# A decoder layer in fp32r halves: another order of work at the ends of parts, at the entry and in the tail

## The reference, cut to what matters

```python
x = x + 0.5 * swiglu(rmsnorm(x, ffn1_norm), ffn1_gate, ffn1_up, ffn1_down)   # 2048 -> 5632 -> 2048
u = rmsnorm(x, mix_norm) @ w_in                       # 8 projections: 4 differential heads, 8 stick-breaking heads
x = x + concat(diff_attention(u), stick_breaking(u)) @ w_out
x = x + 0.5 * swiglu(rmsnorm(x, ffn2_norm), ffn2_gate, ffn2_up, ffn2_down)
x = rmsnorm(x, final_norm)
```

## Time and profile before

| | us |
|---|---|
| median of 3 runs (lowest, highest) | 1858.45 (1858.03, 1859.05) |
| the profiled execution, its own time | 1858.01 |
| span of its trace, first to last instruction | 1856.2 |
| TensorE busy (share) | 1840.0 (99%) |
| VectorE busy | 1029.1 (55%) |
| ScalarE busy | 834.2 (45%) |
| GpSimd busy | 16.1 (1%) |
| mean granted TensorE clock | 0.998 |
| share of time of the 16 transfer engines | 58% |

### The profile page before, as it was taken

How to read it: one execution, slowest core, us unless ns; L and a number is a source line. 1 busy time by engine, 2 the same in 40 slices (tenths; PEclk the granted TensorE clock), 3 DMA queues, 4 the chain that set the end, 5 groups by cost and what they waited for, 6 DMA issues and landing times.

```text
span 1856.2 us, 21845 instructions
## 1 busy us (share of the span) xinstructions
PE 1840.0 (99%) x8490; PEld 1532.9 (83%) x8490; DVE 1029.1 (55%) x1135; ACT 834.2 (45%) x1059; POOL 16.1 (1%) x18
## 2 busy tenths in 40 slices
PE   9999999999999999999999999999999999999998
PEld 7888788888888887888888888888888888888887
DVE  6555545455545457655665576555544555554565
ACT  6434333444334445554656445434333434343444
POOL 0000000000000000101000000000000000000000
PEclk9999999999999999999999999999999999999999
DMA  8656555555656646654445466656565556566653
GB/s 315 208 197 213 193 192 198 196 195 196 224 187 210 206 155 217 216 177 163 159 162 179 147 217 216 213 197 212 193 202 189 195 196 208 198 236 221 201 169 115
DMA packets 230445, 365.78 MB, mean 197 GB/s; under 512 B 13920, under 2 KB 91488, under 8 KB 230368
## 3 DMA queue, kind: packets, MB, share of 16 engines
q1 hardware_dynamic: 229792, 363.78, 58.2%
q10 hardware_dynamic: 576, 0.96, 0.1%
HBM read 346.85 MB, written 2.10 MB: 188 GB/s over the span
## 4 chain that ended last, share of the span: by engine, by line
PE 56%; issue 38%; SPq 2%; DVE 2%; DMA 1%; POOL 0%; ACT 0%; POOLq 0%; DVEq 0%
PE psum L1549 46%; PE psum L1451 5%; PE psum L1456 2%; SPq L414 2%; DMA w_raw<-in_ffn_up 1%; DVE w_split L892 0%; DMA lo_sum<-head_out 0%; DVE x_res L1402 0%; POOL head_rstd L496 0%; DVE x_res L1091 0%; DVE head_out L1127 0%; PE psum L1679 0%; SPq L462 0%; PE psum L1725 0%; PE psum L1694 0%
## 5 line engine op out<-in xcount | busy, mean ns | idle before, releaser
L892 DVE TENSOR_TENSOR w_split<-w_raw,w_split 128x1024 fp32r<-128x1024 f32 (+1 forms) x656 | 764.8, 1207 | 614.3 <-ACT w_split L531 612.8
L1549 PE MATMUL psum<-w_split,x_split 128*128 128x512 f32 x4752 | 1083.7, 390 | 1.8 <-DVE w_split L973 1.8
L531 ACT ACTIVATE w_split<-w_raw 128x1024 fp32r<-128x1024 f32 (+1 forms) x660 | 656.2, 1042 | 920.3 <-PE psum L1549 875.6
L1549 PEld LDWEIGHTS psum<-w_split,x_split 128*128 128x128 f32 x4752 | 891.0, 188 | 187.2 <-DVE w_split L973 2.6
L1549 PE MATMUL psum<-w_split,h_split 128*128 128x512 f32 x2208 | 503.5, 389 | 2.5 <-DVE h_split L1018 2.2
L1549 PEld LDWEIGHTS psum<-w_split,h_split 128*128 128x128 f32 x2208 | 413.9, 188 | 90.1 <-issue 3.7
L1451 PE MATMUL psum<-x_split,w_split 128*128 128x512 f32 x256 | 80.0, 396 | 0.0
L1044 DVE SCALAR_TENSOR_TENSOR strip_sum<-psum,rstd_tok,normed 128x512 f32<-128x512 f32 x44 | 31.0, 747 | 45.5 <-PE psum L1549 45.5
L1456 PEld LDWEIGHTS psum<-x_split,w_split 128*128 128x128 f32 x256 | 46.9, 188 | 10.6
L1451 PE MATMUL psum<-h_split,w_split 128*128 128x512 f32 x168 | 51.8, 395 | 0.0
L1456 PE MATMUL psum<-x_split,w_split 128*128 128x256 f32 x256 | 49.1, 278 | 0.0
(11 more groups left out here) (180 smaller groups left out, 553.8 us busy)
## 6 DMA issues: line engine op xcount, KB each, us to landing
w_raw<-in_ffn_gate SPq DMA_DIRECT2D x87, 1024.0 KB, 5.1
w_raw<-in_ffn_up SPq DMA_DIRECT2D x87, 1024.0 KB, 5.2
w_raw<-in_ffn_down SPq DMA_DIRECT2D x76, 1024.0 KB, 5.1
w_raw<-in_w_in SPq DMA_DIRECT2D x48, 512.0 KB, 4.7
w_raw<-in_w_in SPq DMA_DIRECT2D x24, 1024.0 KB, 5.1
w_raw<-in_w_out SPq DMA_DIRECT2D x16, 1024.0 KB, 5.1
lo_sum<-head_out SPq DMA_DIRECT2D x480, 32.0 KB, 1.9
w_raw<-in_ffn_down SPq DMA_DIRECT2D x16, 768.0 KB, 4.7
```

Of the source, the lines that this page charges most:

```text
L531: nc.scalar.activation(w_split[:, slot % 2, 0, h * half:(h + 1) * half], w_raw[:, slot, h * half:(h + 1) * half], ACT.Copy).then_inc(hi_ma ...
L892: nc.vector.tensor_tensor(w_split[:, slot % 2, 1, part], w_raw[:, slot, part], w_split[:, slot % 2, 0, part].bitcast(F32), ALU.subtract).t ...
L1549: ins = mm(psum[:, bank + t, :], x[:, a, t * P:(t + 1) * P], w[:, b, k, :], start=kk == 0 and (a, b) == (0, 0), stop=kk == count - 1 and a ...
```

## The change

It does the following.

- **Entry.** Two dummy products in place of three. `first_pair` takes high x high, low x high, high x low (x's half is named first), and waits for x's low half and the weights' low half only where they are used. Chunk 2 comes in two halves with a semaphore each; ScalarE and VectorE split chunk 2, then chunk 3.
- **Moves.** At the end of an all-moved part SP issues 12 of the 16 small transfers and ScalarE the other 4 (`move_last_quarter`), ahead of its next conversion.
- **Parts of three chunks.** In VectorE's list `x_from_moved` of the group before now stands after the new delta and the chunk's low half at `q == 2`; `group_norm` on ScalarE and `group_x_lo`, `group_sums` on VectorE stand later by a group, and in the mixer's first chunk groups 2 and 3 are done one by one (`group_high`, `group_squares`).
- **Norm.** VectorE adds the two rows of `square_sum` (`fold_sum`), and TensorE takes two products in place of four, in all norms but the last.
- **Tail.** VectorE scales blocks 3 to 15 in six parts. TensorE spreads the factor into a second bank as well, ScalarE copies it to SBUF, and GpSimd scales blocks 0 to 2 with it (`POOL_PART`). ScalarE issues their output before its last part's.

The diff without its unchanged lines and the two semaphore declarations, indented less:

```diff
@@ -230,7 +230,8 @@
-OUT_PARTS = ((0, 1), (1, 3), (3, 6), (6, 9), (9, 12), (12, 14), (14, 16))
+OUT_PARTS = ((3, 4), (4, 6), (6, 9), (9, 12), (12, 14), (14, 16))
+POOL_PART = (0, 3)
@@ -406,10 +409,10 @@
-        def move_turned(count):
+        def move_turned(count, quarters=4):
...
-            for q in range(4):
+            for q in range(quarters):
@@ -431,7 +434,7 @@
-                    move_turned(count)
+                    move_turned(count, 3 if ph["g0"] is not None and ph["all_moved"] and count == ph["last_moved"] else 4)
@@ -464,8 +467,13 @@
-                for w in range(2):
-                    group_chunk(0, j + w)
+                if j == 2:
+                    dst = w_raw[:, 2, :].rearrange("p (k n) -> p k n", n=2 * STRIP)
+                    for h, done in enumerate((half_landed, landed[2])):
+                        sp.dma_start(dst[:, 2 * h:2 * h + 2, :], source(0, 1)[:, 2 * h:2 * h + 2, :]).then_inc(done, 16)
+                else:
+                    group_chunk(0, j)
+                group_chunk(0, j + 1)
@@ -484,7 +492,7 @@
-    sp.wait_ge(out_written, 16 * len(OUT_PARTS))
+    sp.wait_ge(out_written, 16 * (len(OUT_PARTS) + 1))
@@ -518,6 +526,11 @@
+    pool.wait_ge(x_hi_made, 8 * NORM_FINAL + NS)
+    pool.wait_ge(norm_ready, 2)
+    lo, hi = POOL_PART
+    nc.gpsimd.tensor_tensor(x_blocks[:, lo:hi, :], x_blocks[:, lo:hi, :],
+                            rstd[:, :].unsqueeze(1).broadcast_to([P, hi - lo, T]), ALU.mult).then_inc(pool_scaled, 1)
@@ -561,7 +574,7 @@
-            act.wait_ge(squares_added, q + n)
+            act.wait_ge(squares_added, q + 2 * n)
@@ -595,13 +608,16 @@
-    for c in (2, 3):
-        act.wait_ge(landed[c], 16)
-        act.wait_ge(entry_used, c - 1)
-        hi_part(c, c, HALF_K, 0)
-    for c in (2, 3):
-        act.wait_ge(chunk_used, c + 1)
-        hi_part(c, c, HALF_K, 1)
+    act.wait_ge(half_landed, 16)
+    act.wait_ge(entry_used, 1)
+    hi_part(2, 2, HALF_K, 0)
+    act.wait_ge(landed[2], 16)
+    act.wait_ge(chunk_used, 3)
+    hi_part(2, 2, HALF_K, 1)
+    act.wait_ge(landed[3], 16)
+    act.wait_ge(chunk_used, 4)
+    for h in range(2):
+        hi_part(3, 3, HALF_K, h)
@@ -652,6 +668,25 @@
+    def group_high(ph, i):
+        act.wait_ge(res_done, ph["r0"] + i + 1)
+        for j in range(2):
+            x_hi_parts(2 * i + j, ph["norm"])
+    def group_squares(ph, i):
+        n = ph["norm"]
+        for j in range(2):
+            if i < 3:
+                act.wait_ge(squares_added, 8 * n + 2 * i + j + 2 * n)
+            nc.scalar.activation((normed if i == 3 else squares)[:, j, :, :], x_res[:, 2 * i + j, :, :],
+                                 ACT.Square).then_inc(squared, 1)
+    def move_last_quarter(count):
+        act.wait_ge(hidden_32, count)
+        for a in range(4):
+            act.dma_start(hidden_moved[96:128, a, :, :, :], turned_32[32 * a:32 * a + 32, 3, :, :, :]).then_inc(hidden_landed, 16)
@@ -660,18 +695,22 @@
+                elif i + q == 0:
+                    move_last_quarter(ph["last_moved"])
...
-                if q == 2 and i and ph["norm"] is not None:
+                if ph["norm"] is not None and ph["chunks"] == 4 and q == 2 and i:
...
+                if ph["norm"] is not None and ph["chunks"] == 3 and q == 0 and i > 1:
+                    group_norm(ph, i - 2)
...
-            act.wait_ge(squares_added, 8 * n + NS - 1 + n)
+            act.wait_ge(squares_added, 8 * n + NS - 1 + 2 * n)
@@ -860,9 +899,13 @@
+                if cc == 0:
+                    group_high(ph["after"], 2)
...
-                    group_norm(ph["after"], 3)
+                    group_high(ph["after"], 3)
+                    group_squares(ph["after"], 2)
+                    group_squares(ph["after"], 3)
@@ -872,6 +915,12 @@
+        if n == 0:
+            act.wait_ge(norm_spread_done, 3)
+            nc.scalar.activation(rstd[:, :], psum[:, 7, 0:T], ACT.Copy).then_inc(norm_ready, 1)
+        if n == 5:
+            act.wait_ge(pool_scaled, 1)
+            act.dma_start(out_t[:, slice(*POOL_PART), :], x_blocks[:, slice(*POOL_PART), :]).then_inc(out_written, 16)
@@ -910,13 +959,17 @@
-        dve.wait_ge(squares_added, q + n + 1)
+        dve.wait_ge(squares_added, q + 2 * n + 1)
...
+    def fold_sum(n):
+        dve.wait_ge(squares_added, 10 * n + 9)
+        nc.vector.tensor_tensor(square_sum[:, 0, :], square_sum[:, 0, :], square_sum[:, 1, :], ALU.add).then_inc(squares_added, 1)
@@ -966,12 +1019,8 @@
-    for h in range(2):
-        for c in (2, 3):
-            dve.wait_ge(hi_made, 4 + 2 * h + c - 1)
-            part = slice(h * 4 * STRIP, (h + 1) * 4 * STRIP)
-            nc.vector.tensor_tensor(w_split[:, c % 2, 1, part], w_raw[:, c, part], w_split[:, c % 2, 0, part].bitcast(F32),
-                                    ALU.subtract).then_inc(lo_made, 1)
+    for c in (2, 3):
+        lo_parts(c, c, HALF_K)
@@ -1069,6 +1118,7 @@
+                    fold_sum(0)
@@ -1078,6 +1128,8 @@
+        if i == 3:
+            fold_sum(ph["norm"])
@@ -1117,7 +1169,7 @@
-                if q == 1 and i and ph["turns"]:
+                if i and ph["turns"] and q == (ph["chunks"] - 1 if ph["chunks"] == 3 else 1):
@@ -1134,7 +1186,7 @@
-                if q == 0 and i > 1 and ph["norm"] is not None:
+                if q == (1 if ph["chunks"] == 3 else 0) and i > 1 and ph["norm"] is not None:
@@ -1375,9 +1427,9 @@
+                    group_x_lo(ph["after"], 2)
...
-                    group_x_lo(ph["after"], 2)
@@ -1408,7 +1460,7 @@
-    for _ in range(3):
+    for _ in range(2):
@@ -1477,14 +1529,15 @@
-        pe.wait_ge(squares_added, 9 * n + (8 if n == NORM_FINAL else 9))
+        pe.wait_ge(squares_added, 10 * n + (8 if n == NORM_FINAL else 10))
...
+        parts = 2 if n == NORM_FINAL else 1
...
-            for b in range(2):
-                ins = add(square_sum[:, b, :], t, b == 0, n != NORM_FINAL and b == 1)
+            for b in range(parts):
+                ins = add(square_sum[:, b, :], t, b == 0, n != NORM_FINAL)
@@ -1532,13 +1585,13 @@
-    def wide_chunk(c, slot, bank, quarter, left=None, count=KB, waits=None, during=None, second_lo=1):
+    def wide_chunk(c, slot, bank, quarter, left=None, count=KB, waits=None, during=None):
...
-                pe.wait_ge(lo_made, lo_value(c) - 1 + k // 2 * second_lo)
+                pe.wait_ge(lo_made, lo_value(c) - 1 + k // 2)
@@ -1556,12 +1609,15 @@
-            pe.wait_ge(x_ready if k % 2 else entry_x_ready, k // 2 + 1)
...
-                pe.wait_ge(*((lo_made, LO_CREDIT + 4) if k == 3 and w else (entry_lo, 2 * k + w + 1)))
+                pe.wait_ge(*((hi_made, 4) if k == 3 and w else (entry_hi, 2 * k + w + 1)))
...
-                for a, b in ((0, 0), (0, 1), (1, 0)):
+                for a, b in ((0, 0), (1, 0), (0, 1)):
+                    if a and w == 0:
+                        pe.wait_ge(x_ready if k % 2 else entry_x_ready, k // 2 + 1)
+                    if b:
+                        pe.wait_ge(*((lo_made, LO_CREDIT + 4) if k == 3 and w else (entry_lo, 2 * k + w + 1)))
@@ -1571,7 +1627,7 @@
-            wide_chunk(j, j, 2 * (j % 2), j // 2, waits=x_waits(0) if j % 2 == 0 else None, second_lo=2 if j == 2 else 1)
+            wide_chunk(j, j, 2 * (j % 2), j // 2, waits=x_waits(0) if j % 2 == 0 else None)
@@ -1785,10 +1841,11 @@
-    for b in range(2):
-        ins = mm(psum[:, 6, b * P:(b + 1) * P], rstd_tok[:, b:b + 1].broadcast_to([P, P]), const("ident"),
-                 start=True, stop=True)
-    ins.then_inc(norm_spread_done, 1)
+    for bank in (6, 7):
+        for b in range(2):
+            ins = mm(psum[:, bank, b * P:(b + 1) * P], rstd_tok[:, b:b + 1].broadcast_to([P, P]), const("ident"),
+                     start=True, stop=True)
+        ins.then_inc(norm_spread_done, 1)
```

More of the change, by code:

```diff
@@ L243, in hybrid_layer @@
         piece_landed = [sem(f"piece_landed{n}") for n in range(6)]
+        half_landed = sem("half_landed")
         x_block_landed = [sem(f"x_block_landed{n}") for n in range(2)]
@@ L282, in hybrid_layer @@
         out_ready = sem("out_ready")
+        pool_scaled = sem("pool_scaled")
         lam_ones = sem("lam_ones")
```

## The result

| | before | changed |
|---|---|---|
| median, us | 1858.33 | 1849.06 |
| lowest to highest (5 runs each) | 1858.03 to 1859.05 | 1848.72 to 1849.40 |
| ratio, 95% interval | | 0.995 (0.9939 to 0.9962) |
| profiled execution: its time, span | 1858.01, 1856.2 | 1849.11, 1847.3 |
| TensorE busy | 1840.0 | 1837.7 |

It is faster by 9.3 us, 0.50%. The forecast was 1850.8 with 1849.3 as its low end: the direction was right and the forecast mechanisms show in the rows, but more was won than the range allowed.

What follows compares the result with a forecast made beforehand. TensorE was busy 1840.0 of 1856.2 us, so only its idle or needless time could be won. Gains 2.4 + 1.2 + 2.2 + 1.9 + 0 = 7.7 off 1858.01, plus 0.44 for the median: 1850.8 us, range 1849.3 to 1854.5.

Steps and rivals of the forecast that it cites:

- The stock of stalls: TensorE's four listed waits in places the change touches: 5.9 us, nearly all stalls ahead of the tail.
- the moves: Ends of all-moved parts: with 12 issues SP is through 2.5 us earlier, removing three waits; gain 2.2 us, bounds 0 and 2.2.
- the seam: Third part into mixer: delta ahead of the moved addition, ready 2 us before the turn; gain 1.9 us, bounds 1.2 and 1.95.
- Median: 0.44 us added at the end: the profiled execution was 1858.01, the median of the runs shown 1858.45.
- Norm sums: Four records in place of eight at three norms, 0.4 us each; gain 1.2 us, bounds -0.3 and 1.2.
- Tail: Output scaling: counted at zero because the output's transfers set the end; bounds -0.3 and +0.87 us.
- Entry: Kernel start: first product 0.80 us earlier, chunk 4 at 27.3 instead of 29.7; gain 2.4 us, bounds 1.2 and 3.0.
- ScalarE's share of the issues: End of an all-moved part: its four issues, 2.5 us, fall in 3.49 us of idle time; it resumes about 188.6.
- Rival A: Small transfers: both queues together take no less than one did, the moves gain nothing: 1853.0 us; chance 0.12.
- C: Tail: GpSimd's multiplication is slow, each us beyond 3.6 delays the end; at 6 us 1853.2; chance 0.04.
- D: Entry: chunk 2's first half lands no earlier, chunk 4 at 28.5, entry gain 1.2: 1852.0 us; chance 0.10.
- B: Entry: TensorE's clock rise slips, products cost 0.43 instead of 0.23 us; eight such give 1851.8, all 96 1869; chance 0.10.

Runs made afterwards that it cites:

- u_moves: The changed kernel with SP issuing all 16 small transfers again and ScalarE none: 1852.33 us, 3.3 slower than the changed kernel.
- u_fold: The changed kernel without the fold, TensorE's norm sums taking eight records again at three norms: 1850.44 us, 1.4 slower.
- u_tail: The changed kernel with the tail put back (VectorE scales all 16 blocks, no GpSimd, no copy, one spread): 1849.11 us, the same.
- u_entry: The changed kernel with the whole entry put back (three dummies, old product order, chunk 2 whole, halves by turns): 1851.21 us, 2.15 slower.
- u_half: The changed kernel with chunk 2 in one transfer again, all else kept: 1850.47 us, 1.4 slower.

## Why the prediction was wrong, point by point

- **The stock of stalls** was the mis-sized term, and the step that failed. The forecast took the lines of the earlier trace rows as the cost of the stalls: 2.2 for the moves and 1.9 for the seam. In the profiled executions they cost 3.20 and 2.44, by the starts of products. Each listed stall was undercounted by about 0.25 us, and small losses (0.18 at one place of before, 0.36 ahead of the mixer with the seam back) were not listed at all. That is 1.54 us. u_moves shows it at four places. That records overlap was known ahead of the forecast, and was not applied to the waits.
- **Range.** For the moves I took 2.2 as the upper bound, the sum of the list, and for the seam 1.95. A bound read from a list that undercounts is no bound, and so the low end stood 0.24 us too high. So small a distance is within the tenths by which sets differ; the 1.7 us from the forecast to the measured time is not.
- **Median.** I added 0.44, the distance of before's profiled execution from its median. That execution happened to be faster than all five runs of before; the changed kernel's was 0.05 above its median. This is 0.49 of the 1.74 us by which the forecast missed, and it is chance.
- **Norm sums**: 0.45 each instead of 0.40, 0.14 in all; the mechanism as forecast (u_fold).
- **Tail**: VectorE's first scaling to the end is 8.0 us in both, as forecast, and u_tail prices the split at nothing. The forecast did not have the clock over the spread: 0.49 us lost in the profiled execution. Surplus 1.54 and 0.14, less 0.49 there, and the median's 0.49, make 1.68 of the miss of 1.74; rounding the forecast up to 1850.8 is 0.05 more. The lost half microsecond in the tail hid part of the error in the stalls, by luck.
- **Entry**: right for these executions to 0.01 us (2.40), and each start within 0.2; that the sum is so exact is luck, since the norm sums' start moves by 0.6 us between executions, and over them the gain is 2.2 (u_entry). u_half puts the half at 0.9 to 1.4 (1.2 forecast).
- **ScalarE's share of the issues**: right, at 186.01 it lost nothing. Rival A fell by the queues' timelines, C by GpSimd's 1.81 us, D by ScalarE's start at 13.70. B did not happen in the changed kernel's profile (0.34 us from the first product to the second, 0.23 from there on), and it did for two to four products in four other executions with two dummies.
- **Seam**: the mechanism was right, and the delta was ready 1.6 us before the turn where I had said 2.

## What to carry to other kernels

Price a stall on a pipelined engine from the starts of its instructions on either side, against their spacing when nothing waits, and not from the list of waits: here every listed stall cost 0.2 to 0.3 us more, and some had no line. Many small transfers cost their issue time (0.6 us each here), and a second queue takes its share side by side when its engine has the room. When an order written by hand is changed in two places, price them together and apart: with one line of this seam in its old place, the kernel was 9.6 us slower.

## What was not expected of the hardware

- With no dummies the first products ran 0.43 us apart and then 0.23. With two dummies they were 0.23 apart from the second one on in some executions, and in four of ten the first two to four were still slow; three dummies gave no more certainty.
- In five of the twelve profiled executions without a filling dummy the clock fell in the 1.0 us in which TensorE waits for the last power, and in the others during the spread or after it; it makes 0.5 us. With the filling dummy it fell during the spread in one of two.
- Out of 448 to 480 issues of a 32 KB transfer on SP, 4 to 7 took 0.86 to 1.85 us in every profiled execution, where their neighbours took 0.59. One of 1.52 us made the stall of before's first part 1.36 us instead of about 0.4.
